# The last down-projection unit of an expert kernel, loaded by output columns, and the final norm scaled from memory

## What is computed

```python
def expert_block(args):
    xs, e = args
    gu = xs @ w_gu[e] + b_gu[e]
    gate, up = gu[:, :D_FF], gu[:, D_FF:]
    gate = jnp.minimum(gate, SWIGLU_LIMIT)
    up = jnp.clip(up, -SWIGLU_LIMIT, SWIGLU_LIMIT)
    act = gate * jax.nn.sigmoid(SWIGLU_ALPHA * gate) * (up + 1)
    return act @ w_dn[e] + b_dn[e]
...
y = moe_ffn(h.reshape(-1, d), ...)      # weighted sum over the 4 experts of a token
x = x + g_f * y.reshape(bsz, seq, d)
return rms_norm(x, final_norm_g)        # x * rsqrt(mean(x^2) + eps) * g
```

## Time and profile before

| | before |
|---|---|
| median of 3 runs | 1151.7 us (1150.42 to 1151.74) |
| the profiled execution | 1152.76 us |
| its span, first to last instruction | 1151.0 us |
| PE busy in the span | 968.4 us (84%) |
| DVE, ACT busy | 357.1 us (31%), 243.4 us (21%) |
| moved by DMA | 467.30 MB, mean 406 GB/s |

### The profile page before, as it was taken

How to read it: one execution, slowest core, us unless ns; L and a number is a source line. 1 busy time by engine, 2 the same in 40 slices (tenths; PEclk the granted TensorE clock), 3 DMA queues, 4 the chain that set the end, 5 groups by cost and what they waited for, 6 DMA issues and landing times.

```text
span 1151.0 us, 24523 instructions
## 1 busy us (share of the span) xinstructions
PE 968.4 (84%) x10075; PEld 543.7 (47%) x10076; DVE 357.1 (31%) x801; ACT 243.4 (21%) x365; POOL 8.5 (1%) x28
## 2 busy tenths in 40 slices
PE   7989999998996876889889898898876876876885
PEld 5789999754442432444344444443332432332332
DVE  3689796571221111122121121221211211211112
ACT  3435444531110110011111110110100100100112
POOL 0010000000000000000000000000000000000000
PEclk9989999999999998999999999999898998998898
DMA  9999788999999999999999999999999999999996
GB/s 358 379 337 356 290 317 311 418 387 430 426 429 426 429 426 428 428 428 427 429 426 430 426 430 426 430 427 429 429 427 429 427 428 428 429 426 428 428 426 247
DMA packets 56141, 467.30 MB, mean 406 GB/s; under 512 B 5180, under 2 KB 6260, under 8 KB 27444
## 3 DMA queue, kind: packets, MB, share of 16 engines
q1 hardware_dynamic: 55872, 466.65, 97.8%
q10 hardware_dynamic: 244, 0.29, 0.1%
HBM read 465.87 MB, written 1.05 MB: 406 GB/s over the span
## 4 chain that ended last, share of the span: by engine, by line
PE 46%; DMA 39%; SPq 5%; DVE 4%; issue 4%; ACT 0%; PEld 0%; another core or an unknown queue 0%; PEldq 0%; DVEq 0%; ACTq 0%
PE B L1411 25%; DMA trio<-in_w_down_dram 18%; DMA W<-in_w_down_dram 14%; PE B L1099 10%; DMA W<-in_w_gate_up_dram 4%; PE B L1433 3%; PE B L1422 3%; SPq L414 2%; PE B L1357 2%; DMA raw<-in_w_in_dram 2%; DMA spare<-in_w_ada_dram 2%; SPq L418 1%; PE B L1363 1%; DVE wl L749 1%; PE B L1464 0%
## 5 line engine op out<-in xcount | busy, mean ns | idle before, releaser
L1411 PE MATMUL B<-W,trio 128*32 128x512 f32 (+1 forms) x4784 | 453.5, 522 | 68.8 <-DMA W<-in_w_gate_up_dram 52.9
L1411 PEld LDWEIGHTS B<-W,trio 128*32 128x32 f32 x4784 | 176.9, 110 | 312.4 <-issue 157.8
L667 ACT ACTIVATE EW<-EW 128x256 f32<-128x256 f32 x46 | 19.2, 416 | 680.2 <-DVE EW L1029 680.2
L1029 DVE TENSOR_SCALAR EW<-B 128x256 f32<-128x256 f32 x46 | 19.5, 424 | 447.3 <-PE B L1411 447.3
L1099 PE MATMUL B<-hh,wh 128*128 128x256 f32 x384 | 110.4, 288 | 4.7 <-DVE wl L749 4.7
L1422 PE MATMUL B<-b_gu,trio 128*32 128x256 f32 x736 | 55.4, 410 | 67.1 <-issue 55.6
L1099 PE MATMUL B<-hl,wh 128*128 128x256 f32 x384 | 109.8, 286 | 0.0
L1099 PE MATMUL B<-hh,wl 128*128 128x256 f32 x384 | 109.8, 286 | 0.0
L749 DVE TENSOR_TENSOR wl<-raw,wh 128x2048 fp32r<-128x2048 f32 (+1 forms) x36 | 73.3, 2073 | 18.7 <-ACT wh L562 18.2
L562 ACT ACTIVATE wh<-raw 128x2048 fp32r<-128x2048 f32 (+1 forms) x36 | 60.2, 1719 | 85.0 <-DMA raw<-in_w_in_dram 54.9
L1099 PEld LDWEIGHTS B<-hh,wh 128*128 128x128 f32 x384 | 74.9, 195 | 5.1 <-issue 4.4
(11 more groups left out here) (245 smaller groups left out, 693.6 us busy)
## 6 DMA issues: line engine op xcount, KB each, us to landing
W<-in_w_gate_up_dram SPq DMA_DIRECT2D x112, 2048.0 KB, 34.2
W<-in_w_down_dram SPq DMA_DIRECT2D x48, 2048.0 KB, 37.3
spare<-in_w_gate_up_dram SPq DMA_DIRECT2D x16, 2048.0 KB, 26.9
trio<-in_w_down_dram SPq DMA_DIRECT2D x15, 2048.0 KB, 40.5
raw<-in_w_in_dram SPq DMA_DIRECT2D x12, 2048.0 KB, 10.1
raw<-in_w_ada_dram SPq DMA_DIRECT2D x9, 2048.0 KB, 10.2
raw<-in_w_in_dram SPq DMA_DIRECT2D x4, 1024.0 KB, 15.6
raw<-in_w_out_dram SPq DMA_DIRECT2D x2, 2048.0 KB, 9.0
```

The source lines that it names most:

```text
L667: A(sg, gs, ACT.Sigmoid, scale=ALPHA).then_inc(sig_ready, 1)
L1029: V.tensor_scalar(halves(gs), paired(GU[:, 0:QC]), LIMIT, None, ALU.min).then_inc(gmin_ready, 1)
L1411: t = M(o, src[:, k % KQ, CAP * (k // KQ):CAP * (k // KQ) + CAP], w, start=(first and k == 0), stop=(k == KT - 1))
```

## The change

The last unit is loaded in two blocks of output columns: block c holds columns 512c to 512c+511 of all four k steps. In memory that is four pieces of 2 KB per partition. TensorE runs the four k steps for column groups 0 and 1 behind the first landing, and for groups 2 and 3 behind the second. The weighting of every round becomes two instructions on 64 partitions each, the first behind a new semaphore `down_half`; `yw_ready` counts by two. The last scatter runs by halves of the columns. The squares and the products with the gain are made for each bank as it is complete, the sums and roots for both token blocks in one instruction each, and the last scaling reads the products from SBUF: VectorE scales one whole token block and half of the other, ScalarE the remaining half. There are three stores in place of four.

```diff
+        dn_cols = w_down[0].rearrange("e (h p r) (c n) -> e h c p r n", h=2, p=P, c=NH)
...
-            for g, s_half in enumerate((s_unit[u % SLOTS], s_last)):
-                sp.dma_start(unit_pair(u)[:, g, :], dn_v[e, 1, :, g, :]).then_inc(s_half, 16)
+            for c, s_half in enumerate((s_unit[u % SLOTS], s_last)):
+                sp.dma_start(unit_pair(u)[:, c, :].rearrange("p (r n) -> p r n", n=HALF), dn_cols[e, 1, c]).then_inc(s_half, 16)
...
+            sp.wait_ge(o_ready, 1)
+            sp.dma_start(out[0, 0:P, :], HV[:, 0, :]).then_inc(s_out, 16)
+            sp.wait_ge(o_ready, 2)
+            sp.dma_start(out[0, P:2 * P, HALF:2 * HALF], HV[:, 1, HALF:2 * HALF]).then_inc(s_out, 16)
...
+            for n, (h, a) in enumerate(((0, 0), (0, 1), (1, 0), (1, 1))):
                 act.wait_ge(y_all, n + 1)
+                if a == 1:
+                    act.wait_ge(xg_ready, 2 * h + 1)
...
+                A(squares[n], Yb[a][h][:, :], ACT.Square,
+                  accum_out=stat[:, SS3 + 2 * a + h:SS3 + 2 * a + h + 1]).then_inc(x3_sq, 1)
...
+            A(HV[:, 1, 0:HALF], HV[:, 1, 0:HALF], ACT.Copy, scale=stat[:, RST3 + 1:RST3 + 2]).then_inc(oa_ready, 1)
...
+                dve.wait_ge(down_half, n + 1)
+                V.tensor_tensor(yw[0:2 * CAP, :], Db[0:2 * CAP, 0:QC], gfq[0:2 * CAP, :], ALU.mult).then_inc(yw_ready, 1)
                 dve.wait_ge(down_done, n + 1)
-                V.tensor_tensor(yw, Db[:, 0:QC], gfq, ALU.mult).then_inc(yw_ready, 1)
+                V.tensor_tensor(yw[2 * CAP:P, :], Db[2 * CAP:P, 0:QC], gfq[2 * CAP:P, :], ALU.mult).then_inc(yw_ready, 1)
...
+            for h, a in ((0, 1), (0, 0), (1, 1), (1, 0)):
+                dve.wait_ge(y_all, 2 * h + a + 1)
+                if a == 0:
+                    dve.wait_ge(x3_sq, 2 * h + 1)
+                V.tensor_tensor(HV[:, a, halves_of[h]], Yb[a][h][:, :], gfin[:, halves_of[h]], ALU.mult).then_inc(xg_ready, 1)
...
+            for a, cs in enumerate((slice(0, D), halves_of[1])):
+                V.tensor_scalar(HV[:, a, cs], HV[:, a, cs], stat[:, RST3 + a:RST3 + a + 1], None, ALU.mult).then_inc(o_ready, 1)
...
+                if split:
+                    u = u0 + 1
+                    pe.wait_ge(s_unit[u % SLOTS], 16 * (USES * turns + unit_uses(u)))
+                    for c in range(NH):
+                        if c == 1:
+                            pe.wait_ge(s_last, 16)
+                        for k in range(KT - per, KT):
+                            for g in (2 * c, 2 * c + 1):
+                                at = HALF * (k % per) + QC * (g % 2)
+                                t = M(dst[CAP * g:CAP * g + CAP, :], src[:, k % KQ, CAP * (k // KQ):CAP * (k // KQ) + CAP],
+                                      unit_pair(u)[:, c, at:at + QC], start=False, stop=(k == KT - 1))
+                        if c == 0:
+                            t.then_inc(down_half, 1)
...
+            def scatter_last(n):
+
+                for h in range(NH):
+                    pe.wait_ge(yw_ready, 2 * n + 1 + h)
+                    pe.wait_ge(spread_out, 2 * NQ * n + NQ)
+                    for a in range(TA):
+                        scatter_into(a, h, 2 * h + a, spread_out)
+                    pe.wait_ge(spread_out, 2 * NQ * n + NQ + TA * (h + 1))
+                    for a in range(TA):
+                        scatter_into(a, h, 2 * h + 1 - a, y_all)
...
-            wait_outputs(n)
-            scatter(n, last=True)
+            scatter_last(n)
```

More of the change, by code:

```diff
@@ L473, in _ @@
             sp.dma_start(gfin, final_norm_g[:].partition_broadcast(P)).then_inc(s_gfin, 16)
[L474 to L478, removed]
+            sp.wait_ge(o_ready, 1)
+            sp.dma_start(out[0, 0:P, :], HV[:, 0, :]).then_inc(s_out, 16)
+            sp.wait_ge(o_ready, 2)
+            sp.dma_start(out[0, P:2 * P, HALF:2 * HALF], HV[:, 1, HALF:2 * HALF]).then_inc(s_out, 16)
+            sp.wait_ge(s_out, 16 * 3)
         @block.gpsimd
@@ L681, in _ @@
             A(stat[:, WARM:WARM + 1], stat[:, VVAR:VVAR + 1], ACT.Sqrt).then_inc(act_step, 1)
-            squares = [EW[:, 0:HALF], mod[:, 2, :], EW[:, 2 * HALF:3 * HALF], HV[:, 0, HALF:2 * HALF]]
-            def square(n):
+            squares = [EW[:, 0:HALF], EW[:, 2 * HALF:3 * HALF], mod[:, 2, :], EW[:, 0:HALF]]
+            act.wait_ge(c_eps, 1)
+            for n, (h, a) in enumerate(((0, 0), (0, 1), (1, 0), (1, 1))):
                 act.wait_ge(y_all, n + 1)
[L687 to L706, removed]
+                if a == 1:
+                    act.wait_ge(xg_ready, 2 * h + 1)
+                if n == 3:
+                    act.wait_ge(x3_sq, 1)
+                A(squares[n], Yb[a][h][:, :], ACT.Square,
+                  accum_out=stat[:, SS3 + 2 * a + h:SS3 + 2 * a + h + 1]).then_inc(x3_sq, 1)
+            act.wait_ge(x3_var, 1)
+            A(stat[:, STD3:STD3 + TA], stat[:, VAR3:VAR3 + TA], ACT.Sqrt, scale=1.0 / D,
+              bias=stat[:, EPS_AT:EPS_AT + 1]).then_inc(x3_std, 1)
+            act.wait_ge(rst_ready, 1)
+            act.wait_ge(xg_ready, TA)
+            A(HV[:, 1, 0:HALF], HV[:, 1, 0:HALF], ACT.Copy, scale=stat[:, RST3 + 1:RST3 + 2]).then_inc(oa_ready, 1)
             act.wait_ge(oa_ready, 1)
-            act.dma_start(out[0, P:2 * P, cs], HV[:, 1, cs]).then_inc(s_out, 16)
+            act.dma_start(out[0, P:2 * P, 0:HALF], HV[:, 1, 0:HALF]).then_inc(s_out, 16)
         @block.vector
@@ L1053, in _ @@
             halves_of = [slice(h * HALF, (h + 1) * HALF) for h in range(NH)]
[L1054 to L1079, removed]
+            for h, a in ((0, 1), (0, 0), (1, 1), (1, 0)):
[3 more added lines that the diff above has]
+                V.tensor_tensor(HV[:, a, halves_of[h]], Yb[a][h][:, :], gfin[:, halves_of[h]], ALU.mult).then_inc(xg_ready, 1)
+            dve.wait_ge(x3_sq, TA * NH)
+            V.tensor_tensor(stat[:, VAR3:VAR3 + TA], stat[:, SS3:SS3 + 4:2], stat[:, SS3 + 1:SS3 + 4:2], ALU.add).then_inc(x3_var, 1)
+            dve.wait_ge(x3_std, 1)
+            V.reciprocal(stat[:, RST3:RST3 + TA], stat[:, STD3:STD3 + TA]).then_inc(rst_ready, 1)
+            dve.wait_ge(rst_ready, 1)
+            dve.wait_ge(xg_ready, TA * NH)
+            for a, cs in enumerate((slice(0, D), halves_of[1])):
+                V.tensor_scalar(HV[:, a, cs], HV[:, a, cs], stat[:, RST3 + a:RST3 + a + 1], None, ALU.mult).then_inc(o_ready, 1)
         @block.tensor
@@ L1396, in stream @@
                 per = KQ if rows_of is gate_up_row else 2 * KQ
-                for k in range(KT):
+                for k in range(KT - per if split else KT):
                     u = u0 + k // per
@@ L1412, in stream @@
                               start=(first and k == 0), stop=(k == KT - 1))
+                        if rows_of is down_row and k == KT - 1 and g == 1:
+                            t.then_inc(down_half, 1)
                     if k % per == per - 1 and k < KT - 1:
                         t.then_inc(released, 1)
+                if split:
[10 more added lines that the diff above has]
+                        if c == 0:
+                            t.then_inc(down_half, 1)
                 return t
@@ L1423, in bias, with scatter_into, scatter @@
                           sel[:, NH * s + g // 2, :], pairs[:, :, g % 2, :], start=(s == 0), stop=False)
-            def scatter(n, last=False):
+            def scatter_into(a, h, g, signal):
+                rows_ = slice(CAP * g, CAP * g + CAP)
+                M(Yb[a][h][:, (g % 2) * QC:(g % 2) * QC + QC], SwT[rows_, a * P:(a + 1) * P], yw[rows_, :],
+                  start=False, stop=True, skip_group_check=True).then_inc(signal, 1)
+            def scatter(n):
                 for q in range(2):
@@ L1430, in scatter @@
                         for h in range(NH):
[L1431 to L1434, removed]
+                            scatter_into(a, h, 2 * h + (q + a) % 2, spread_out)
+            def scatter_last(n):
[7 more added lines that the diff above has]
+                        scatter_into(a, h, 2 * h + 1 - a, y_all)
             def wait_outputs(n):
-                pe.wait_ge(yw_ready, n + 1)
+                pe.wait_ge(yw_ready, 2 * n + 2)
                 pe.wait_ge(swT_ready, n + 1)
```

8 lines of the change are left out of this document (3 added, 5 removed).

## The result

| | before | after |
|---|---|---|
| median of 20 executions each | 1151.59 us (1149.51 to 1154.73) | 1153.28 us (1151.30 to 1156.70) |
| ratio | | 1.0015, 95% interval 1.0010 to 1.0021 |
| the profiled execution, its span | 1152.76, 1151.0 us | 1153.55, 1151.8 us |

The changed kernel is slower by 1.7 us (1.15 to 2.4), which is 0.15%. The forecast was 1153.0.

What follows compares the result with a forecast made beforehand. Up to the last expert the weight stream sets the time; behind it each step counts. 0.44 + 0.87 + 0 - 0.16 + 0.41 - 0.3 = +1.26 us on 1151.7 gives 1153.0, range 1150.8 to 1154.8.

Steps and rivals of the forecast that it cites:

- Part 1: The last unit's two loads: 2 KB pieces are read slower than 8 KB, last landing +0.44 us (0 to 0.65).
- Part 2: Matmuls behind each landing: time goes by k steps, not records, so 1.99 us for the block, +0.87 behind the last landing.
- Rival (b): Last unit: matmul time goes by records (1.12 us) and 2 KB pieces cost nothing; -0.05 us, 1151.6, chance 0.13.
- Part 3: Split weighting: covered in the rounds; TensorE's way out of the loop ends last, so 0, lower bound -0.35 us.
- Rival (c): Last round: the first half's scatter runs under the second transfer, one step of 0.88 less; +0.38 us, 1152.1, chance 0.02.
- Part 4: Last scatter: three dependent steps at 2.4 GHz take 2.55 us where two took 2.71, -0.16; at 1.2 GHz +1.39.
- rival (a): The clock falls before the scatter: +2.41 us, 1154.1, or 1155.8 with the burst; chance 0.25, 0.07 of it with the burst.
- Part 5: Final norm and stores: first output 3.45 us after the scatter, +0.41; stores issued close together, -0.3.
- The term of 0.40: Final norm: VectorE's two products of the first half reach 0.40 us past the scatter, part of the +0.41.

Runs made afterwards that it cites:

- e1: The changed kernel with the last unit loaded and multiplied by halves of the rows again, all else kept; 1152.06 us, ratio 1.0008 to the kernel before.
- e2: The changed kernel with both column blocks' matmuls behind the second landing, on all four column groups; 1153.40 us, ratio 1.0012 to the kernel before.
- e7: The changed kernel with the first half's scatter moved ahead of the wait for the second landing; 1154.22 us, ratio 1.0026 to the kernel before.
- e5: The kernel before with the new norm and stores, the split weighting, and the second scatter step ordered by column halves; 1152.77 us, ratio 1.0013.
- e6: The kernel before with only the weighting split into two instructions of 64 partitions in all 46 rounds; 1151.93 us, ratio 1.0005.
- e3: The kernel before with each half of the last unit's rows fetched in two transfers of 2 KB pieces, matmuls as before; 1152.42 us, ratio 1.0004.
- e11: The kernel before, unchanged, a second additional profiled execution for the clock of the scatter; 1151.98 us.
- e9: The kernel before with the last unit in three loads by rows (two k steps, one, one), without filler matmuls; 1151.03 us, ratio 0.9999.
- e10: The kernel before, unchanged, one additional profiled execution for the clock of the scatter; 1151.55 us.
- e4: The kernel before with unused matmuls on TensorE, five ahead of the wait for the last landing and three behind the last burst; 1151.78 us, ratio 1.0002.
- e8: The kernel before with the last unit in three loads by rows, three unused matmuls ahead of the last wait and three behind the last burst; 1151.85 us, ratio 1.0002.
- e12: The changed kernel, unchanged, one additional profiled execution for the clock of the scatter; 1153.09 us.

## Why the prediction was right

Time, sign and mechanism came as forecast; the sum, 1.26 us, was 0.4 us short of the medians, inside their interval. One term, the scatter, was mis-sized. The low end of the range, 1150.8, should by its own terms (1151.0 less 0.35) have been 1150.65; nothing hangs on it.

**Part 1, the landing.** +0.36 and +0.39 in two kernels, forecast +0.44, and the rate beside it (387 GB/s) as read from the w_in loads (392). The landings say the same without TensorE's start in the measure: from the landing of the unit before to the last landing are 4.9 to 5.0 us in the nine profiles without 2 KB pieces (before: 1096.98 + 36.2 to 1138.13) and 5.2 to 5.3 in the four with the column blocks (after: 1095.69 + 37.2 to 1098.3 + 39.9), some 0.3 later. The rule of 3 cycles per packet in the Trainium skill ("DMA: Bandwidth & Descriptors", section "Why small descriptors are slow (HBM only)") from which I had estimated +0.17 is too small here: the row of the slow stretch was the better guide. What I did not see is that SP is held by the issue (below).

**Part 2, the matmuls.** 1.92 for four k steps on two column groups, 1.93 on four. Rival (b) falls, since its 1.12 did not come; e1 and after differ by 0.84, forecast 0.87. The Trainium skill's rule for narrow matmuls ("TensorE: Matmul & The Clock Gate", section "Why this matters for your kernels") agrees with these numbers. Choosing the step and not the record as the unit was right, though the only row for it was one on row groups.

**Part 3, the weighting and the exit.** The way out stayed, 0.86 us against 0.85 (0.81 by the chain's rows, which end the burst 0.04 later), and the early weighting of the first half brought at most 0.1: e2, without it, has the same time. Rival (c) falls twice: the first scatter stands behind the second burst, and where it is put ahead of it (e7) it makes the burst late instead.

**Part 4, the scatter.** Right for the changed kernel: three dependent steps, 2.46 us at granted clock 1.00, in both profiles of it (and in e1 and e2), so rival (a) did not come in these. The clock was partly luck. I chose 1.00 because TensorE is busier before the scatter, but the profiles do not bear that reason out: e5, with before's two bursts and 1.4 us between them, kept 1.00 as well, and e1, with the short bursts, had it too.

The size that was off is that of *before*. I took its 2.71 (2.63 to the last record's end) from one profiled execution as if the kernel always ran it so. Of seven profiles with the old order of two steps and no filler, the scatter took 2.63 (before), 2.63 (e6), 2.30 (e3), 2.27 (e11), 1.72 (e9), 1.59 (e10) and 1.58 (e5), on average 2.10. Against that the new order's 2.46 costs +0.36 and does not give 0.16. With it the sum is 1.26 + 0.16 + 0.36 = 1.78, beside a measured 1.7. From the scatter's start to the first output the three profiles of before itself have 5.75, 5.38 and 4.71 us, after has 5.94; with the other differences of the table (+0.36 + 0.86 - 0.28) the change costs 1.13, 1.50 and 2.17 us by the one or the other, 1.6 on average, and the interval of the comparison, 1.15 to 2.4, holds this spread nearly whole. That this is what moves the medians is worked out from single profiles, not shown by an experiment that sets the clock. The two with filler (e4, e8) got the short scatter and no shorter time; e4 lost about 1 us ahead of it, and e8 speaks against the explanation as far as its interval goes.

**Part 5, the norm.** First output 3.48 us after the scatter's last record, where the forecast's 3.45, which starts 0.08 later, would be 3.53; 3.12 to 3.48 is +0.36, forecast +0.41. The second executions (e10 to e12) have 3.12, 3.11 and 3.49. The stores took 4.07, forecast 4.05. The term of 0.40 by which VectorE's products reach past the scatter is seen in e5 at its other end: with no cover the norm costs 4.45 - 3.12 = 1.3 more. The reason, read from the rows and not tested by itself, is the order: the old norm made one product and then one token block's sum, root and inverse, while the other block's squares ran; the new one makes four products, in turns with ScalarE's four squares, before its one sum. Squares and products end together (the last square's sum is read by 1145.46, the last product ends at 1145.50); how much of the cost is the products and how much the two engines' waits for each other, no run separates. Writing the outputs from memory faster (1.15 us for both instructions) did not give that back.

## What to carry to other kernels

Work done early is only worth something if the engine that ends last can use it early without being late for its next work. Here TensorE's program order put the first half's scatter behind the second half's matmuls, where it was put ahead (e7) those matmuls came late, and the smaller blocks were paid in full (shorter pieces, twice the k steps behind the last landing). Cut the last transfer along the dimension that leaves fewer steps behind it (rows, so k steps), not along one in which the array is parallel anyway. And before a step at the end of a kernel is priced, look at it in several executions: the clock that one profile shows there need not be the kernel's.

## What the runs showed of the hardware that I had not expected

**Issuing many small pieces holds the issuing engine.** In the changed kernel the two loads of 2 KB pieces (512 pieces each) took these times to issue on SP (ns, min, median, max):

```profile
L471 SPq DMA_DIRECT2D trio<-in_w_down_dram x2: 568/5678/10788, 1097.5 to 1098.3; - x2
```

The second took 10.8 us, where a load of 128 pieces of 8 KB takes 0.33. The next load on the queue is the final gain vector's. In before SP waited 8.7 us for a release and issued it at 1108.98; in the changed kernel that wait is gone from its profile, and the issue at 1109.75 comes 0.7 us behind the end of the hold (1097.53 + 11.54). It was free here: the vector landed at about 1139.4 in both, and its first use is at 1142.66. With four loads of 256 pieces each (e3, 24.4 us) it was issued at 1123.3 and landed at 1139.7. With a weight load behind it the hold could have been on the path; that was not tried.

**When the clock falls near the end varies from execution to execution.** With the same rounds, it fell to 0.50 between 1127 and 1132 in four of the profiles (e1, e4, e7, e10), at 1139.4 to 1141 in five (before, e3, e6, e9, e11), and only behind the scatter in the other five. TensorE's idle stretches do not sort them: e5, e6 and e11 all have about 1.4 us between the last two bursts, and their scatters run at 1.00, at 0.50 and at both. An early fall makes TensorE late for the last unit (x32 burst at 1135.15 in e10, 1133.58 before), though the landings stay about 2.5 us apart (1135.6 and 1138.1 in e10); a fall ahead of the scatter makes the scatter 2.63 us in place of 1.59. What decides between them the runs do not show.
